# Normalizing retention heads inside the retention, and starting the output projection in the last gated units, in a three-block transformer kernel

## The reference

```python
def rms_norm(x, g): return x * rsqrt(mean(x * x) + EPS) * g
def first_block(x):
    for l in range(2):                       # the entry is the first line at l = 0
        x = x + 0.5 * swiglu(rms_norm(x, ffn_norm_g[l, 0]), ffn_w_gate[l, 0], ffn_w_up[l, 0], ffn_w_down[l, 0])
...
def token_mixing(h_lat, h_ctx, w_in):        # second block, 4 retention and 4 GLA heads of 128
    # o_ret: retention, forward and backward, over context then latent tokens
    # o_gla: gated linear attention, forward and backward, log gates from log_sigmoid
    mu, var = mean(o_ret), mean((o_ret - mu) ** 2)
    r  = (o_ret - mu) * rsqrt(var + EPS) * ret_norm_w * silu(p[3])
    gl = o_gla * rsqrt(mean(o_gla ** 2) + EPS) * gla_norm_w * silu(p[7])
    return concatenate([r, gl]) @ w_out
```

## Time and profile before

| | us |
|---|---|
| median of three runs | 3643.57 |
| the profiled execution, its own time | 3629.36 |
| its span | 3627.6 |
| PE busy in the span | 3495.7 (96%) |
| DVE, ACT, POOL busy | 1681.7, 1478.7, 1524.2 |

### The profile page before, as it was taken

The page is one execution under the profiler, slowest core; times in us unless marked ns, Lnnn a source line. Parts: engine busy times, 40 slices in busy tenths (PEclk is TensorE's granted clock), DMA queues, the critical chain, the costliest instruction groups (busy, mean ns, idle before and its releaser), DMA issues.

```text
span 3627.6 us, 56429 instructions
## 1 busy us (share of the span) xinstructions
PE 3495.7 (96%) x21462; PEld 2933.4 (81%) x21462; DVE 1681.7 (46%) x2790; ACT 1478.7 (41%) x2449; POOL 1524.2 (42%) x1352
## 2 busy tenths in 40 slices
PE   7999999999999999999999999999999999889998
PEld 6999776689998999776689997888887785658887
DVE  7456634575657456634575655111113304651112
ACT  5444434554545444434554544312113335243223
POOL 3555544445545555543445543323333431024443
PEclk9999999999999999999999999999999999989999
DMA  4333343323333343443323332222212332013331
GB/s 121 105 110 89 95 129 115 96 64 110 106 92 94 101 114 87 103 124 115 96 64 110 107 91 89 64 64 64 64 57 59 88 89 74 1 47 100 97 99 64
DMA packets 569041, 322.57 MB, mean 89 GB/s; under 512 B 30266, under 2 KB 563360, under 8 KB 568480
## 3 DMA queue, kind: packets, MB, share of 16 engines
q1 hardware_dynamic: 568864, 320.22, 31.0%
HBM read 318.08 MB, written 2.10 MB: 88 GB/s over the span
## 4 chain that ended last, share of the span: by engine, by line
PE 68%; issue 17%; POOL 7%; DVE 4%; ACT 2%; SPq 1%; DMA 0%; POOLq 0%; ACTq 0%; DVEq 0%
PE psum L2737 21%; PE psum L2653 17%; PE psum L2824 12%; POOL w_lo L917 6%; PE psum L3019 2%; PE psum L3091 2%; PE psum L3050 2%; PE psum L2993 1%; PE psum L3342 1%; PE psum L3114 1%; PE psum L2664 1%; PE psum L2862 1%; PE psum L3130 1%; PE psum L2758 1%; PE psum L2761 1%
## 5 line engine op out<-in xcount | busy, mean ns | idle before, releaser
L917 POOL TENSOR_TENSOR w_lo<-w_raw,w_hi 128x512 fp32r<-128x512 f32 x488 | 659.6, 1374 | 1160.6 <-ACT w_hi L1005 1160.6
L1005 ACT ACTIVATE w_hi<-w_raw 128x1024 fp32r<-128x1024 f32 x244 | 257.7, 1058 | 871.5 <-PE psum L2653 746.0
L2653 PE MATMUL psum<-h_hi,w_hi 128*128 128x512 f32 x1184 | 471.6, 398 | 2.4 <-POOL w_lo L917 2.1
L2653 PE MATMUL psum<-h_hi,w_lo 128*128 128x512 f32 x1184 | 462.4, 391 | 0.0
L2653 PE MATMUL psum<-h_lo,w_hi 128*128 128x512 f32 x1184 | 462.3, 390 | 0.0
L968 POOL TENSOR_TENSOR set_lo<-w_raw,set_hi 128x512 fp32r<-128x512 f32 x224 | 294.0, 1341 | 223.1 <-ACT set_hi L1068 220.1
L2737 PE MATMUL psum<-t_hi,set_hi 128*128 128x256 f32 x1280 | 364.1, 284 | 13.8 <-issue 7.7
L2737 PE MATMUL psum<-t_hi,set_lo 128*128 128x256 f32 x1280 | 363.3, 284 | 0.0
L2737 PE MATMUL psum<-t_lo,set_hi 128*128 128x256 f32 x1280 | 363.3, 284 | 0.0
L2824 PE MATMUL psum<-a_hi,set_hi 128*128 128x512 f32 x704 | 274.5, 390 | 2.8 <-DVE a_lo L1937 2.8
L2824 PE MATMUL psum<-a_lo,set_hi 128*128 128x512 f32 x704 | 274.0, 389 | 0.0
(11 more groups left out here) (562 smaller groups left out, 7943.5 us busy)
## 6 DMA issues: line engine op xcount, KB each, us to landing
w_raw<-ffn_w SPq DMA_DIRECT2D x120, 512.0 KB, 3.9
w_raw<-ffn_w_gate SPq DMA_DIRECT2D x88, 512.0 KB, 4.1
w_raw<-ffn_w_up SPq DMA_DIRECT2D x88, 512.0 KB, 4.0
ada_raw<-ada_w SPq DMA_DIRECT2D x72, 512.0 KB, 4.7
w_raw<-ffn_w_down SPq DMA_DIRECT2D x64, 512.0 KB, 4.5
w_raw<-w_in SPq DMA_DIRECT2D x60, 512.0 KB, 3.9
w_raw<-ffn_w_down SPq DMA_DIRECT2D x32, 384.0 KB, 3.7
w_raw<-w_out SPq DMA_DIRECT2D x24, 512.0 KB, 4.1
```

The costliest lines, as they stand in the source:

```text
L917: last = nc.gpsimd.tensor_tensor(w_lo[:, i, at], w_raw[:, i, at], w_hi[:, i, at].bitcast(F32), ALU.subtract)
L1005: nc.scalar.activation(w_hi[:, pos, :], w_raw[:, pos, :], ACT.Copy).then_inc(hi_ready, 1)
L2653: last = nc.tensor.matmul(dst, w[:, pos, k * P:(k + 1) * P], rhs[g][r](k0 + k), start=k == 0 and m == 0, stop=k == nk - 1 and m == 2)
```

## The change

At the entry the gains of the first norm have a small transfer and a transpose of their own ahead of x (bank 7), and the others are turned by PE after the second tile and copied by DVE after the root. All four weight slots are requested before them. The norm's squares are no longer added on DVE: PE adds each of the 8 over the partitions with a matmul of its own, between the blocks of the first tile. DVE's constants move behind the first and the second pair of units.

In the second block retention heads are centred, normed and gated while the retention and the states run; ACT's copies of the level matrices and of the doubled queries go to DVE. The level sums of a unit are split, two banks before the second half of the scores and two behind. The output blocks 0 to 3 take their first four rows of heads in units 6 and 7 and between the GLA norms, in banks that stay open; the last four rows go head by head over the four blocks, and blocks 4 to 7 follow whole, each in a bank of its own.

```diff
+NORM_BANK = (6, 7, 6, 2)
+OUT_BANK = (0, 1, 4, 5, 6, 7, 2, 3)
...
-factors = [over(f"factors_{i}", [P, 2 * (LEVELS + 1), P], at) for i, at in enumerate((h_at + 16384, h_at + 24576, log_gates_at + 8192))]
+factors = [over(f"factors_{i}", [P, 2 * (LEVELS + 1), P], at) for i, at in enumerate((log_gates_at + 8192, h_at + 24576, h_at + 16384))]
-inv_2 = over("inv_2", [P, 2, T], rope_at)
+ret_root = [over(f"ret_root_{i}", [P, T], at) for i, at in enumerate((h_at + 30720, rstd_at))]
...
 @block.sync
     sp.dma_start(ident[:], a["c_ident"]).then_inc(x_rows_loaded, 16)
+    sp.dma_start(gain_rows[0:KD, :], a["ffn_norm_g"][0][0].rearrange("(r p) -> r p", p=P)).then_inc(x_rows_loaded, 16)
     sp.dma_start(x_rows[:], a["x"][0].rearrange("(t p) d -> p t d", p=P)).then_inc(x_rows_loaded, 16)
-    gate_and_up(0, 0, ffn_gate[0], ffn_up[0], True, range(2))
+    gate_and_up(0, 0, ffn_gate[0], ffn_up[0], True)
...
-    gate_and_up(0, 0, ffn_gate[0], ffn_up[0], True, range(2, SLOTS))
...
 @block.scalar
-    for i in range(2):
-        down_high(0, i)
+    nc.scalar.activation(credits[:, 16:17], eps[:], ACT.Copy)
+    down_high(0, 0)
     act.wait_ge(gains_ready, 1)
-    for c in range(KD - 1):
+    for c in range(KD):
         b_high(0, 0, 0, c, lambda c: next_gains[:, c:c + 1])
-        square(0, 0, 0, c, rows)
+        if c:
+            square(0, 0, 0, c - 1, rows)
+        if c == 1:
+            down_high(0, 1)
...
+    def root_of_head(g):
+        act.wait_ge(*latent_sum(LAST, g + 1))
+        if g >= 2:
+            act.wait_ge(merged, g - 1)
+        nc.scalar.activation(ret_root[g % 2][:], psum[:, NORM_BANK[g], :], ACT.Abs_reciprocal_sqrt, bias=eps[:, 0:1], scale=1.0 / P).then_inc(latent_std.sem, 1)
+        act.wait_ge(*latent_std(LAST, 2 * g + 1))
+        nc.scalar.activation(rk[:, g, :], ret_root[g % 2][:], ACT.Square, scale=(0.5 / P) ** 0.5).then_inc(latent_std.sem, 1)
     for h in range(RET_H + 1):
...
-        if h == 3:
+        if h == 1:
             gate_logs()
+        if h >= 2:
+            root_of_head(h - 2)
+        if h:
+            act.wait_ge(centred, h)
+            nc.scalar.activation(rk[:, h - 1, :], rq[:, h - 1, :], ACT.Square).then_inc(latent_sq.sem, 1)
+        if 1 <= h < RET_H - 1:
+            nc.scalar.activation(credits[:, 17:18], eps[:], ACT.Exp)
...
-    nc.scalar.activation(q_twice[:], gq[:], ACT.Copy, scale=2.0)
...
-    for b in range(4):
-        nc.scalar.activation(sums_f[:, at], sums_raw[0][:, at], ACT.Copy).then_inc(sums_act_ready, 1)
+    root_of_head(RET_H - 1)
...
+    for g in range(RET_H):
+        head_high(g)
     copy_gla(*units()[UNITS - 2])
+    act.wait_ge(gla_o_ready, UNITS - 1)
+    gla_square(0)
+    gla_square(1)
+    gla_root(0)
+    copy_gla(*units()[UNITS - 1])
+    act.wait_ge(gla_o_ready, UNITS)
+    gla_square(2)
+    gla_square(3)
+    for j in range(1, GLA_H):
+        gla_root(j)
+        head_high(RET_H + j - 1)
+    head_high(RET_H + GLA_H - 1)
...
 @block.vector
     for c in range(KD - 1):
...
         b_low(0, 0, 0, c, lambda c: next_gains[:, c:c + 1])
-        if c:
-            norm_add(0, 0, c, T)
...
     inverse_root(layer, v, [(0, T)], 2)
+    if not layer and not j:
+        copy_gains()
...
     set_last_low(turn + 1, next_gate, 0)
-    settled()
     set_sums_of(turn + 1, next_up, 1, (layer, copies + 1))
+    joined(next_gate, 0, silu_1[1])
...
+    if q == 1 and not layer and not j:
+        constants_ready()
+        dve.wait_ge(*cond_ready(0, 0))
...
+    if q == 2:
+        settled()
...
+    def gate_head(g):
+        o, gate, _, _, _ = of_head(g)
+        dve.wait_ge(*latent_sq(LAST, g + 1))
+        nc.vector.scalar_tensor_tensor(o, o, merge_gains[:, g:g + 1], gate, ALU.mult, ALU.mult).then_inc(latent_normed.sem, 1)
+    def scale_head(g):
+        o, _, bank, root, half = of_head(g)
+        dve.wait_ge(*latent_std(LAST, 2 * g + 2))
+        nc.vector.scalar_tensor_tensor(half, psum[:, bank, :], P * EPS, half, ALU.add, ALU.mult).then_inc(latent_root.sem, 1)
+        dve.wait_ge(*latent_root(LAST, 2 * g + 1))
+        nc.vector.scalar_tensor_tensor(root, half, 1.5, root, ALU.subtract, ALU.mult).then_inc(latent_root.sem, 1)
+        dve.wait_ge(*latent_root(LAST, 2 * g + 2))
+        dve.wait_ge(*latent_normed(LAST, g + 1))
+        nc.vector.tensor_tensor(o, o, root, ALU.mult).then_inc(merged, 1)
     for h in range(RET_H):
...
-        if h == 3:
+        if h == 1:
...
+        if h >= 1:
+            centre(h - 1)
+        if h >= 2:
+            gate_head(h - 2)
+            scale_head(h - 2)
+    centre(RET_H - 1)
+    gate_head(RET_H - 2)
+    scale_head(RET_H - 2)
+    gate_head(RET_H - 1)
...
+    for raw, sums in zip(sums_raw, (sums_f, sums_b)):
+        for b in range(4):
+            nc.vector.tensor_copy(sums[:, at], raw[:, at]).then_inc(sums_dve_ready, 1)
+    nc.vector.tensor_scalar(q_twice[:], gq[:], 2.0, None, ALU.mult)
     for t in range(TT + TCT):
...
+        if t == TCT:
+            scale_head(RET_H - 1)
...
     for n, c, p in units():
         gla_merge(n, 0)
         if n + 1 < UNITS:
             gla_factors(*units()[n + 1])
-        else:
-            centre(0)
-            centre(1)
+        if n == UNITS - 2:
+            dve.wait_ge(gla_o_done, UNITS - 2)
+            for g in range(RET_H):
+                merge_low(g)
         gla_merge(n, 1)
-    for h in range(2 * RET_H):
...
+    for g in range(RET_H, 2 * RET_H):
+        gate_head(g)
+        scale_head(g)
+        if g > RET_H:
+            merge_low(g - 1)
...
 @block.tensor
+    nc.tensor.transpose(psum[:, KD - 1, 0:KD], gain_rows[0:KD, :], ident[0:KD, 0:KD]).then_inc(rows_turned, 1)
     for c in range(KD):
-        if c == GAINS_AT:
-            pe.wait_ge(gains_loaded, GAINS * 16)
...
+    def first_sum(c):
+        pe.wait_ge(*sq_ready(0, c + 1))
+        last = nc.tensor.matmul(psum[:, 2, :], minus[:], squares_1[:, c % 2, :], start=c == 0, stop=c == KD - 1)
...
 +            if first_norm and k:
+                first_sum(k - 1)
...
+        elif i == 1 and first_norm:
+            pe.wait_ge(gains_loaded, GAINS * 16)
+            nc.tensor.transpose(psum[:, 7, 0:70], gain_rows[0:70, :], ident[0:70, 0:70])
+            nc.tensor.transpose(psum[:, 7, P:2 * P], gain_rows_2[:], ident[:]).then_inc(rows_turned, 1)
+            pe.wait_ge(consts_loaded, CONSTS * 16)
...
     for h in range(RET_H):
         if h + 1 < RET_H:
             ret_scores(h + 1)
+        if h:
+            mean(h - 1)
...
+        if h:
+            head_sum(h - 1)
-    pe.wait_ge(ret_o_ready, RET_H)
+    mean(RET_H - 1)
...
-    totals(range(EARLY_TOTALS))
+    totals(range(1))
+    head_sum(RET_H - 1)
+    totals(range(1, EARLY_TOTALS))
...
+    pe.wait_ge(*latent_root(LAST, 2 * (RET_H - 2) + 1))
     suffixes(0)
...
+    def project(c, ks):
+        turn, pos = slot_of(LAST, S_MIX2 + len(SLOTS_2) + c)
+        if ks[0] == 0:
+            pe.wait_ge(lo_ready, turn * SLOTS + (SLOTS + pos + 1))
+        for k in ks:
+            pe.wait_ge(*latent_lo_ready(LAST, k + 1))
+            for m, (w, r) in enumerate(((w_hi, 0), (w_hi, 1), (w_lo, 0))):
+                last = nc.tensor.matmul(psum[:, OUT_BANK[c], :], w[:, pos, k * P:(k + 1) * P], lat[r](k), start=k == 0 and m == 0, stop=k == KD - 1 and m == 2)
+        if ks[-1] == KD - 1:
+            last.then_inc(slot_used, 1)
...
     for n, c, p in units():
         gla_scores(n, c, p, 0)
         if n:
             gla_output(*units()[n - 1])
-        if n == UNITS - 1:
-            pe.wait_ge(factor_exp, UNITS)
-            mean(0)
-            mean(1)
+        if n + 2 < UNITS:
+            gla_sums(*units()[n + 2], range(2))
         gla_scores(n, c, p, 1)
         if n + 2 < UNITS:
-            gla_sums(*units()[n + 2])
+            gla_sums(*units()[n + 2], range(2, 4))
+        if n >= UNITS - 2:
+            pe.wait_ge(factor_exp, UNITS)
+            project(n - (UNITS - 2), range(RET_H))
+    gla_sum(0)
+    gla_sum(1)
     gla_output(*units()[UNITS - 1])
-    for h in range(2 * RET_H + 1):
...
+    project(2, range(RET_H))
+    gla_sum(2)
+    gla_sum(3)
+    project(3, range(RET_H))
+    for k in range(RET_H, KD):
+        for c in range(SLOTS):
+            project(c, range(k, k + 1))
+    for c in range(SLOTS, KD):
+        project(c, range(KD))
     norm_sums(LAST, 3, [(0, T)])
```

More of the change, by code:

```diff
@@ L731, in _ @@
                     src = a[name] if layer is None else a[name][layer]
+                    if row == 0 and dst is gain_rows:
+                        src = src[1:2]
+                        row = KD
                     while len(src.shape) > 1:
```

196 lines of the change are left out of this document (92 added, 104 removed).

## The result

The changed kernel takes 3604.13 us, the median of four runs (3600.85 to 3607.72), against 3644.10 in four runs of the kernel before beside it: a ratio of 0.9893, with a 95% interval of 0.9871 to 0.9916. It is faster by 40 us, and the forecast of 3606 in a range of 3596 to 3622 was right. Six more runs in a second comparison gave 3603.92 and 0.9901 (0.9882 to 0.9920), 37 us.

The account below looks back on a forecast made before the run. PE, busy in 96% of the span, bounds the kernel; only its idle and half-clock time can be won. 11.4 - 6.3 + 3.9 + 28.9 = 37.9, from 3643.6 to 3605.7 us; range 3596 to 3622, 8 in 10.

Parts of the forecast that it names:

- Tail: From unit 6 to the norm's sums: 61.9 us instead of 90.8, so 28.9 gained.
- Entry: From the start to the first down product: 11.4 us gained, by an earlier PE, a shorter hole and full pace.
- DVE would allow more: Entry, first tile: DVE's last low part comes at about 26.3, ahead of PE, which is done at 30.0.
- the hole of 1.4: Entry, at about 54: PE still waits 1.4 us for DVE's chain, where the hole was 6.0.
- I put them at nothing: Entry: DVE's constants, moved to later pairs, cost nothing thanks to DVE's idle time; at most 2.9 us.
- Retention: Second block, up to the first state product: 6.3 us lost to added means and squares, bounds 3 and 9.
- Units: Units 0 to 5: period of 7.5 instead of 8.1 us by the split level sums, 3.9 gained, at most 4.9.
- (a): Rival, entry: PE's clock falls and the entry gains nothing; total gain 26.5, 3617 us; chance 0.12.
- (b): Rival, tail: the four open blocks stall and the clock falls for 96 early matmuls; 19 lost, 3625 us; chance 0.08.
- (d): Rival, slower: new breaks keep PE at 1.2 GHz from unit 6 through the projection; 50.8 lost, 3656 us; chance 0.02.
- (c): Rival, larger gain: retention hides nearly all its sums, tail has no wait at the weights; 3600 to 3597; chance 0.10.
- (e): Rival, entry: x shares DMA engines with two more weight slots and comes 2.5 us later; 3608; no chance given.

Follow-up runs that it names:

- the edit of the last rows: Changed kernel with the last two rows of heads taken block by block over four open output blocks: unit 6 to norm's sums 59.95 us alone, 60.8 with two other edits.
- slot 1's edit: Changed kernel with ACT's high part of weight slot 1 behind block 5 instead of block 1: first unit products at 48.17, 1.6 us earlier; 0.7 reaches the down products.
- The two kernels without the hole of 2.10: Changed kernel with weight slot 1 split behind block 5, alone (second tile at 30.73) and with DVE's constants and last rows moved too (3596.31 us, 0.9883 of the kernel before).

## Why the prediction was right, point by point

**Tail, right in its steps.** Unit 7 began 9.74 after unit 6 (forecast 9.8), blocks 0 to 3 ended at 38.0, the wait for slot 0 was 1.77 (2.1), block 4 began at 40.0 (40.1), the end was at 61.9. The last low parts came at 32 to 33. It held because each wait was followed on the engine that causes it, in DVE's order, and because the projection's pace was read from starts. Part of it is luck with the clock: in three of ten executions it fell in unit 6, and the end was at 62.8 (60.8 with the edit of the last rows).

**Entry, first part right in sum, wrong in its steps.** "DVE would allow more" failed: I took block 2's low parts at their undisturbed length, and POOL's split beside them made 0.42 into 1.48; a wait of 0.88 for ACT's first square was not in the sum either. PE began the blocks at 16.3 and not at 17.4, and the second tile at 32.4, not 30.0. Transposes were faster than the 0.22 taken (32 in 5.94). The late start filled the hole of 1.4 that I expected. The product that stood at 69.18 before stands at 58.08 (49.80 and 69 products at 0.12): 11.1 earlier, forecast 11.4.

**Entry, second part wrong.** From there to the down products 4.7 of the 11.1 were lost, to four waits of 3.8 and a slow restart of about 0.2 after each. The step that failed is "I put them at nothing": the constants cost 1.7, measured. The other 3.0 are put down to DVE's chain, which runs from 41.5 to 68.2 with 1.4 us of idle time; that the old hole of 6 us had let it catch up is argued, not tested. Where the profile names ACT, at 64.64 and 69.30, ACT had itself waited for DVE (0.67 and 2.96 us, at 62.22 and 67.55). That this chain binds is shown at the wait of 60 by slot 1's edit (0.7 of 1.6 arrive); what would shorten it was not tried.

**Retention, mis-sized.** Forecast 5.9 at the transposes, measured 4.6. Heads 1 and 2 cost 1.7 and not 2.6, as head 0's sum went into the wait of 0.78 too; head 3 cost 2.0 (2.3), the last mean 0.9 (1.0). Its wait for ACT's copy came as described, 1.05. Behind the transposes I had 0.4 lost and 0.9 was won: the kernel before made the 8 instructions of the suffixes in 3.7 us at a mean clock of 0.54, the changed one in 2.0 at 1.00. No step of the forecast had this. The wait in front of the state product grew to 1.90 where I had it shrink to 0.5. So 3.7 lost instead of 6.3.

**Units.** The period is 7.67, not 7.5: PE is busy 44.6 of 45.7 us, and no wait of DVE is left; PE's own work bounds it, with 7.67 where I had summed 7.3 (before it was 8.1 less the wait of 0.69, so 7.4, and the split adds the rest). In unit 0 a wait of 0.88 for ACT's factors is left. Won 2.9, not 3.9; the terms of the forecast themselves give 3.8.

**Not in the sum:** 1.6 between the first state product and unit 0, where the mean clock rose from 0.83 to 0.88. It is not safe: in four of the eleven executions with the new second block this piece took 30.8 us again, at 0.83, as before the change.

**Rivals.** (a) came in small: a clock of 0.94 at the entry in six of nine executions, costing 1.3. The two kernels without the hole of 2.10 both had 1.00, which is too few to call the hole its cause. (b) and (d) did not come in the first profile, where the clock is 1.00 throughout the tail; in three later ones it fell for most of the first output block, which cost 0.9 and not 19 or more. (c) was half right on the retention (3.7 lost where the added matmuls are 7.0) and wrong on the wait for weights. The range was said to hold (b) as well, but (b)'s 3625 lies outside it. (e) did not come: x lay 0.1 later. The misses of the entry and the units (5.0 and 1.0 too much) and of retention and level sums (2.6 and 1.6 too little) nearly cancel, and some 3.3 of the latter are the clock. So the total is better than its terms, and that is luck.

## What to carry to other kernels

A hole that is closed may also have been the time in which another engine caught up: follow that engine's chain past the hole until its own idle time, and count only idle time that is not a wait for its own product as room. A vector operation on SBUF, with two inputs above all, is priced by what POOL does beside it. And before two profiles are subtracted, compare a stretch of unchanged code: here it differed by 14 us.
